# Multiplying the second norm's root onto the projections' results, and splitting the input inside the residual block

## The chip, the cores and the metric

The kernel runs on one core of one Trainium2 chip. The metric is the device time of one launch in microseconds; the median of repeated executions is compared. All data are float32. Products of matrices are made in three passes over values that are split into a high half and a low half, so that nearly the full precision is kept.

## The reference, cut to what matters

Two layers of a decoder trunk work on 1024 prompt tokens and 8 sample tokens. In each layer a norm with a gain stands ahead of the mixer's input projection and another ahead of the ConvFFN:

```python
def rmsnorm(x, g):
    y = xf * lax.rsqrt(jnp.mean(xf * xf, axis=-1, keepdims=True) + EPS)
    return y * g

h = rmsnorm(x, norm_mix_pre[layer])
proj = h @ w_in                      # 24 tiles of 128 columns (25 in layer 0)
...                                  # mixer, then mix = ... @ w_out
x = x + rmsnorm(mix, norm_mix_post[layer])
h = rmsnorm(x, norm_ffn_pre[layer])
g = h @ w_gate                       # then a causal convolution along the tokens
a = gelu(conv(g) + b_conv) * (h @ w_up)
x = x + rmsnorm(a @ w_down, norm_ffn_post[layer])
```

The root is one number for each token. It can be multiplied onto `h` ahead of a projection or onto the projection's result.

## The kernel before, in words

The activations lie transposed: 128 channels on the partitions, 1032 tokens (1024 and 8) in a row, eight such tiles `T.acc[:, k, :]` for the 1024 channels. The matrix product of such tiles with a weight tile of 128 columns takes 72 matmuls (8 tiles k, three passes, three chunks of 344 tokens) and fills one of two regions of PSUM, three banks each. `T.hh` and `T.hl` hold the high and low halves of the eight input tiles, `slot_h` and `slot_l` those of four weight tiles.

Every engine has its own program, written out by hand, and waits on semaphores. The work is a row of blocks; a block ends for all engines at once. Four blocks of the kind `stage_norm` are followed by a block that reads the normed input: `nm0` and `nm1` (first norm of a layer) by `stage_project`, `nf0` and `nf1` (second norm of a layer) by `stage_ffn`. `stage_norm` in three of the four (not in `nm0`, where there is no residual yet) does this:

- TensorE sums the squares of the mixer's or ConvFFN's result over the channels (`ones_times`, L128), ScalarE makes the root `rstd` (L135, L136).
- For each tile k: VectorE (even k, L325) or GpSimd (odd k, L338) multiplies with `rstd`; VectorE multiplies with the gain and adds the old x (L329), which gives the new x and counts up `x_new`.
- ScalarE squares the new tile (L313), TensorE adds it to the sum of squares, and SyncE stores it (L297). From k = 4 on, ScalarE makes the high half of one weight tile ahead of each square (L379), and GpSimd its low half (L383).
- ScalarE makes the second root, in `T.sqsum`. That ends the block.

The next block begins with `StageInput`: VectorE multiplies a tile with gain and root into one of two buffers (`scale`, L245), ScalarE makes its high half (L235), VectorE (odd k) or GpSimd (even k) its low half (L239). TensorE's first product follows tile by tile (`ready`). Only then does the stage run at its steady pace. ScalarE is in `stage_project` otherwise busy with splitting weights and, in layer 0, with activations.

In `stage_project` VectorE moves each finished product out of PSUM (`move`, L627). In `stage_ffn` there are eleven groups. TensorE makes, for two tiles t of the hidden layer, the gate (region 0) and the up product (region 1), and after the first pair eight products of the group before with `w_down`, two of these tiles each. Per tile, ScalarE copies the gate out of PSUM (`tile`, L739), VectorE convolves it (five instructions, L879 to L885), ScalarE applies the gelu (L743), VectorE multiplies with the up product from PSUM (L891) and splits the result into halves (L896, L897). VectorE also adds the eight down products to `T.acc` (`collect`, L904). The last group's down products start only when its second tile is split.

Of the kernel before, what the change touches and what calls it, by code (L numbers as in the profile page):

```python
# [24 lines left out]
KD = D // P  # L25
# [191 lines left out]
class StageInput:  # L217

    def __init__(self, nc, T, name, gain_row=None):
        sem = lambda n: nc.alloc_semaphore(name + n)
        self.T, self.gain_row, self.bufs = T, gain_row, None
        self.scaled, self.hi_done = sem("scaled"), sem("hi_done")

        self.lo_done = [sem("lo_done0"), sem("lo_done1")]

    def source(self, k):
        return self.T.acc[:, k, :] if self.gain_row is None else self.bufs[k % 2]  # L230
# [6 lines left out]
    def lo_half(self, eng, k):  # L237
        eng.wait_ge(self.hi_done, k + 1)
        eng.tensor_tensor(self.T.hl[:, k, :], self.source(k), self.T.hh[:, k, :], ALU.subtract  # L239
                          ).then_inc(self.lo_done[k % 2], 1)  # L240

    def scale(self, dve, k):
        if k >= 2:
            dve.wait_ge(self.lo_done[k % 2], k // 2)
        dve.scalar_tensor_tensor(out=self.bufs[k % 2], in0=self.T.acc[:, k, :],  # L245
                                 scalar=self.T.gain[:, k, self.gain_row:self.gain_row + 1], in1=self.T.sqsum[:],
                                 op0=ALU.mult, op1=ALU.mult).then_inc(self.scaled, 1)

    def vector(self, dve):
        if self.gain_row is None:  # L250
            for k in range(KD):
                self.lo_half(dve, k)
        else:
            self.scale(dve, 0)
            for k in range(1, KD, 2):
                self.scale(dve, k)
                if k + 1 < KD:
                    self.scale(dve, k + 1)
                self.lo_half(dve, k)

    def gpsimd(self, pool):
        for k in range(0, KD if self.gain_row is not None else 0, 2):
            self.lo_half(pool, k)
# [5 lines left out]
def stage_norm(nc, T, name, post_row, x_scratch, feed):  # L269
# [3 lines left out]
    with ExitStack() as ctx:  # L273
# [4 lines left out]
        root1, normed, act_own = sem("root1"), sem("normed"), sem("act_own")  # L278
# [4 lines left out]
        with nc.Block() as block:  # L283
# [17 lines left out]
            def _(act):  # L301
# [16 lines left out]
            def _(dve):  # L318
                steps = Steps(dve, dve_own)

                if post:
                    dve.wait_ge(root1, 1)
                    for k in range(KD):
                        if k % 2 == 0:
                            steps.done(dve.tensor_tensor(T.acc[:, k, :], T.acc[:, k, :], rstd[:], ALU.mult))  # L325
                        else:
                            dve.wait_ge(normed, k // 2 + 1)
# [3 lines left out]
                                                 in1=xold[:, k % 4, :], op0=ALU.mult, op1=ALU.add).then_inc(x_new, 1)  # L331

            @block.gpsimd
            def _(pool):
                if post:
                    pool.wait_ge(root1, 1)
                    for k in range(1, KD, 2):
                        pool.tensor_tensor(T.acc[:, k, :], T.acc[:, k, :], rstd[:], ALU.mult).then_inc(normed, 1)  # L338
                feed.first_gpsimd(pool)
# [72 lines left out]
def stage_project(nc, T, name, source, feed, m_tiles, out_scratch=None, tail=None, conv=None):  # L412
# [9 lines left out]
    with ExitStack() as ctx:  # L422
# [4 lines left out]
        source.bufs = [out[:, r, PAD:] for r in range(2)]  # L427
# [31 lines left out]
        with nc.Block() as block:  # L459
# [48 lines left out]
            def _(pool):  # L508
# [22 lines left out]
                source.gpsimd(pool)  # L531
# [13 lines left out]
            def _(act):  # L545
# [20 lines left out]
                for k in range(KD):  # L566
                    source.scalar(act, k)
                    if not fed and k >= KD - feed.SLOTS:
# [14 lines left out]
            def _(pe):  # L583
                def tile(j, i):
# [5 lines left out]
                    for k in range(KD):  # L590
                        if j == 0:
                            source.ready(pe, k)
# [23 lines left out]
            def _(dve):  # L616
                def move(j, i):
# [9 lines left out]
                    dve.tensor_copy(chunks(dst), region(T.ps, j % 2)).then_inc(moved[j], 1)  # L627
# [30 lines left out]
                source.vector(dve)  # L658
                dve.wait_ge(source.lo_done[0], KD // 2)
# [17 lines left out]
def stage_ffn(nc, T, name, source, feed, layer, w_down, w_conv, b_conv, state, out_prompt, out_sample):  # L677
# [3 lines left out]
    with ExitStack() as ctx:  # L681
# [21 lines left out]
        source.bufs = [gate[:, 2:2 + TOK], conv[:]]  # L703
# [3 lines left out]
        with nc.Block() as block:  # L707
# [23 lines left out]
            def _(act):  # L731
# [20 lines left out]
                def group(g, more):  # L752
                    tile(0, g)
# [6 lines left out]
                    tile(1, g)  # L760
# [6 lines left out]
                for k in range(KD):  # L767
                    source.scalar(act, k)
# [10 lines left out]
            def _(pool):  # L779
# [20 lines left out]
                source.gpsimd(pool)  # L800
                pool.wait_ge(source.scaled, KD)
# [3 lines left out]
                group(GROUPS - 1, False)  # L805
                pool.memset(T.sqsum[:], 0.0).then_inc(sqsum_own, 1)
# [5 lines left out]
            def _(pe):  # L812
                def hidden(s, g):
                    pe.wait_ge(lo[s], g + 1)
                    for k in range(KD):
                        if s == 0 and isinstance(g, int) and g == 0:
# [1638 lines left out]
```

## Time and profile before

| | |
|---|---|
| median of 3 runs | 3521.66 us (3521.66 to 3524.58) |
| span of the profiled execution, first to last instruction | 3518.7 us |
| TensorE, busy | 3038.9 us (86%) |
| VectorE, busy | 1600.2 us (45%) |
| ScalarE, busy | 935.1 us (27%) |
| GpSimd, busy | 913.4 us (26%) |
| mean granted TensorE clock | 0.921 |

For the profiled execution only the span is known; the median is 2.96 us more, which is the time around the first and the last instruction. Busy time counts an instruction from its start to its end, also while it waits for a port, and a matmul's end is modelled.
### The profile page before, as it was taken

All of it is one profiled execution on the core that took longest, in us unless ns stands there. A gap on an engine that the chain in (4) does not pass through costs nothing. (4 is left out here: it accounts for less than half of the span.)

```text
span 3518.7 us, 46382 instructions
## 1 busy us (share of the span) xinstructions
PE 3038.9 (86%) x18726; PEld 2906.3 (83%) x18726; DVE 1600.2 (45%) x1858; ACT 935.1 (27%) x1342; POOL 913.4 (26%) x474
## 2 busy tenths in 40 slices
PE   7999478959699999999689956777596999999995
PEld 6999368839599999999579956666494999999995
DVE  3263435432555444444531127777326444444444
ACT  3221433212321211211320015666213212111112
POOL 2221034304432212221422103333045222122113
PEclk9999689969799999999899978888798999999997
DMA  4221300021411111110322122122304111111103
GB/s 161 90 96 52 135 9 0 1 78 48 160 37 61 46 36 54 54 36 12 112 88 96 71 96 96 60 89 72 120 26 160 49 60 36 36 60 48 36 12 98
DMA packets 158134, 235.94 MB, mean 67 GB/s; under 512 B 12625, under 2 KB 124625, under 8 KB 157976
## 3 DMA queue, kind: packets, MB, share of 16 engines
q1 hardware_dynamic: 158060, 234.95, 19.7%
q8 instruction: 46, 0.75, 0.1%
q14 instruction: 28, 0.23, 0.0%
HBM read 176.75 MB, written 58.46 MB: 67 GB/s over the span
## 5 line engine op out<-in xcount | busy, mean ns | idle before, releaser
L904 DVE TENSOR_TENSOR acc<-acc,ps 128x1032 f32<-128x1032 f32 x176 | 216.3, 1229 | 292.1 <-PE ps L119 292.1
L119 PE MATMUL ps<-ffn_in1hi,rest1wh 128*128 128x344 f32 x1056 | 226.0, 323 | 4.2 <-DVE ffn_in1lo L239 3.5
L119 PE MATMUL ps<-ffn_in0hi,rest0wh 128*128 128x344 f32 x1056 | 225.5, 322 | 3.2 <-DVE ffn_in0lo L239 2.9
L119 PE MATMUL ps<-ffn_in1lo,rest1wh 128*128 128x344 f32 x1056 | 225.1, 321 | 0.0
L119 PE MATMUL ps<-ffn_in0lo,rest0wh 128*128 128x344 f32 x1056 | 224.9, 321 | 0.0
L119 PE MATMUL ps<-ffn_in0hi,rest0wl 128*128 128x344 f32 x1056 | 223.8, 320 | 0.0
L119 PE MATMUL ps<-ffn_in1hi,rest1wl 128*128 128x344 f32 x1056 | 223.8, 320 | 0.0
L383 POOL TENSOR_TENSOR rest0wl<-wraw,rest0wh 128x1024 fp32r<-128x1024 f32 x52 | 130.6, 2516 | 306.9 <-ACT rest0wh L379 306.8
L383 POOL TENSOR_TENSOR rest1wl<-wraw,rest1wh 128x1024 fp32r<-128x1024 f32 x52 | 130.4, 2512 | 265.3 <-ACT rest1wh L379 265.0
L119 PEld LDWEIGHTS ps<-ffn_in1hi,rest1wh 128*128 128x128 f32 x1056 | 178.5, 189 | 5.4 <-DVE ffn_in1lo L239 4.1
L119 PEld LDWEIGHTS ps<-ffn_in0hi,rest0wh 128*128 128x128 f32 x1056 | 178.4, 189 | 4.1 <-DVE ffn_in0lo L239 3.5
L119 PEld LDWEIGHTS ps<-ffn_in1lo,rest1wh 128*128 128x128 f32 x1056 | 179.9, 190 | 0.0
L119 PEld LDWEIGHTS ps<-ffn_in0lo,rest0wh 128*128 128x128 f32 x1056 | 179.5, 190 | 0.0
L119 PEld LDWEIGHTS ps<-ffn_in1hi,rest1wl 128*128 128x128 f32 x1056 | 176.8, 189 | 0.0
L119 PEld LDWEIGHTS ps<-ffn_in0hi,rest0wl 128*128 128x128 f32 x1056 | 176.7, 189 | 0.0
L2111 POOL TENSOR_TENSOR wraw<-at_s,at_rc 128x128 f32<-128x128 f32 (+3 forms) x64 | 76.7, 1198 | 256.5 <-DVE at_rc L2055 250.4
L627 DVE COPY poout<-ps 128x1032 f32<-128x1032 f32 x24 | 29.6, 1233 | 234.9 <-PE ps L119 234.9
L119 PE MATMUL ps<-mix_in1hi,in1wh 128*128 128x344 f32 x576 | 123.7, 323 | 13.8 <-POOL mix_in1lo L239 9.1
L119 PE MATMUL ps<-mix_in0hi,in0wh 128*128 128x344 f32 x600 | 129.3, 324 | 4.8 <-DVE mix_in0lo L239 4.4
L119 PE MATMUL ps<-mix_in0lo,in0wh 128*128 128x344 f32 x600 | 128.3, 322 | 0.0
L119 PE MATMUL ps<-mix_in0hi,in0wl 128*128 128x344 f32 x600 | 127.5, 321 | 0.0
L119 PE MATMUL ps<-mix_in1lo,in1wh 128*128 128x344 f32 x576 | 123.0, 322 | 0.0
(434 smaller groups left out, 6871.1 us busy)
## 6 DMA issues: line engine op xcount, KB each, us to landing
wraw<-in_w_ffn_gate SPq DMA_DIRECT2D x22, 1024.0 KB, 5.4
wraw<-in_w_ffn_up SPq DMA_DIRECT2D x22, 1024.0 KB, 5.3
wraw<-in_w_ffn_down SPq DMA_DIRECT2D x22, 1024.0 KB, 4.9
x_scratch<-acc SPq DMA_DIRECT2D x32, 516.0 KB, 7.8
proj_odd<-poout SPq DMA_DIRECT2D x24, 516.0 KB, 2.7
wraw<-in_w_in_even SPq DMA_DIRECT2D x12, 1024.0 KB, 5.6
wraw<-in_w_in_odd SPq DMA_DIRECT2D x12, 1024.0 KB, 5.6
sr_page<-in_cache_k SPq DMA_DIRECT2D x16, 512.0 KB, 5.5
```

The lines of the kernel that those rows point to most:

```text
L119: ins = pe.matmul(ps[:, 3 * r + c, 0:CH], w, h[:, c * CH:(c + 1) * CH], start=first and n == 0, stop=last and n == 2)
L383: pool.tensor_tensor(self.slot_l[j], self.source(j), self.slot_h[j], ALU.subtract).then_inc(self.lo[j], 1)
L627: dve.tensor_copy(chunks(dst), region(T.ps, j % 2)).then_inc(moved[j], 1)
L904: dve.tensor_tensor(a, a, region(T.ps, m % 2), ALU.add).then_inc(collected, 1)
L2111: pool.tensor_tensor(w[:, i % 2, 0:spans[i]], s[:, i % 4, 0, 0:spans[i]], rc[:, i % 4, 0:1].to_broadcast([P, spans[i]]), ALU.mult).then_in ...
```

## The change

The gain is applied when the new x is split, inside `stage_norm`; the second root is multiplied onto the results of the projections. ScalarE makes the high half of `gain * x` directly ahead of the square; VectorE makes the low half one tile later. VectorE also takes over GpSimd's four multiplications with `rstd`. In `stage_project` the copy out of PSUM becomes a multiplication with the root. In `stage_ffn` VectorE takes the gate out of PSUM, with the root, in place of ScalarE, and multiplies the product of gelu and up once more with the root ahead of its split. GpSimd clears `T.acc` at once and `T.sqsum` only after the last split.

```diff
 class StageInput:
     def scalar(self, act, k):
-        if self.gain_row is not None:
-            act.wait_ge(self.scaled, k + 1)
-        act.activation(self.T.hh[:, k, :], self.source(k), ACT.Copy).then_inc(self.hi_done, 1)
         if self.gain_row is None:
+            act.activation(self.T.hh[:, k, :], self.T.acc[:, k, :], ACT.Copy).then_inc(self.hi_done, 1)
         else:
+            act.activation(self.T.hh[:, k, :], self.T.acc[:, k, :], ACT.Copy, scale=self.gain(k)).then_inc(self.hi_done, 1)
+    def vector(self, dve, k):
+        dve.wait_ge(self.hi_done, k + 1)
+        ...
+            ins = dve.scalar_tensor_tensor(out=self.T.hl[:, k, :], in0=self.T.acc[:, k, :], scalar=self.gain(k),
+                                           in1=self.T.hh[:, k, :], op0=ALU.mult, op1=ALU.subtract)
+        ins.then_inc(self.lo_done[k % 2], 1)
...
 def stage_norm(...):                      # ScalarE
                     if post:
                         act.wait_ge(x_new, k + 1)
+                    source.scalar(act, k)
                     if k >= 2:
                         act.wait_ge(summed2, k - 1)
                     act.activation(sq[:, k % 2, :], T.acc[:, k, :], ACT.Square).then_inc(squared, 1)
...                                        # VectorE
-                        if k % 2 == 0:
-                            steps.done(dve.tensor_tensor(T.acc[:, k, :], T.acc[:, k, :], rstd[:], ALU.mult))
-                        else:
-                            dve.wait_ge(normed, k // 2 + 1)
+                        steps.done(dve.tensor_tensor(T.acc[:, k, :], T.acc[:, k, :], rstd[:], ALU.mult))
                         dve.wait_ge(x_in[k % 4], 16 * (k // 4 + 1))
                         dve.scalar_tensor_tensor(...).then_inc(x_new, 1)
+                        if k:
+                            source.vector(dve, k - 1)
+                else:
+                    for k in range(KD - 1):
+                        source.vector(dve, k)
+                source.vector(dve, KD - 1)
...                                        # GpSimd
-                if post:
-                    pool.wait_ge(root1, 1)
-                    for k in range(1, KD, 2):
-                        pool.tensor_tensor(T.acc[:, k, :], T.acc[:, k, :], rstd[:], ALU.mult).then_inc(normed, 1)
...
 def stage_project(...):                   # VectorE
-                    dve.tensor_copy(chunks(dst), region(T.ps, j % 2)).then_inc(moved[j], 1)
+                    if fed:
+                        dve.tensor_tensor(chunks(dst), chunks(T.sqsum[:]), region(T.ps, j % 2), ALU.mult).then_inc(moved[j], 1)
+                    else:
+                        dve.tensor_copy(chunks(dst), region(T.ps, j % 2)).then_inc(moved[j], 1)
...
 def stage_ffn(...):                       # ScalarE
-                def tile(t, g):
-                    act.wait_ge(made[2 * t], g + 1)
-                    act.wait_ge(kept, 2 * g + t)
-                    act.wait_ge(conved, 2 * g + t)
-                    act.activation(chunks(gate[:, 2:2 + TOK]), region(T.ps, 0), ACT.Copy).then_inc(gate_in, 1)
...                                        # GpSimd
-                pool.wait_ge(source.scaled, KD)
                 pool.memset(T.acc[:], 0.0).then_inc(acc_zero, 1)
...
+                pool.wait_ge(a_ready, 2 * GROUPS)
                 pool.memset(T.sqsum[:], 0.0).then_inc(sqsum_own, 1)
...                                        # VectorE
                 def convolve(steps, t, g):
+                    dve.wait_ge(made[2 * t], g + 1)
+                    dve.wait_ge(kept, 2 * g + t)
+                    dve.tensor_tensor(chunks(gate[:, 2:2 + TOK]), chunks(T.sqsum[:]), region(T.ps, 0), ALU.mult
+                                      ).then_inc(gate_in, 1)
                     dve.wait_ge(gate_in, 2 * g + t + 1)
...
                 def split(steps, t, g):
                     dve.wait_ge(multiplied, 2 * g + t + 1)
+                    steps.done(dve.tensor_tensor(conv[:], conv[:], T.sqsum[:], ALU.mult))
                     steps.done(dve.tensor_copy(ah[:, t, :], conv[:]))
```

The calls of `source.scalar`, `source.vector`, `source.gpsimd` and `ready` at the start of `stage_project` (for a normed input) and of `stage_ffn` are gone, and with them `scale`, `lo_half` and the two buffers.

## Rows read from the trace of the kernel before

**Rows 1.** Windows: stretch | us, busy us of PE, PEld, DVE, ACT, POOL, granted clock, DMA.

```profile
1166.00:1266.00 100.00, 100.00 (x635) 100.00 (x634) 50.63 (x36) 16.78 (x14) 20.32 (x10) 1.00 0.13 42
```

**Rows 2.** Timeline, second norm of layer 0: start, us, engine, line, instruction [idle before].

```profile
905.76 1.23 DVE L325 TENSOR_TENSOR acc<-acc,nf0rstd 128x1032 f32<-128x1032 f32 x1 [10.96 <-ACT nf0rstd L136]
...
907.03 6.58 DVE L329 SCALAR_TENSOR_TENSOR acc<-acc,gain,nf0xold 128x1032 f32<-128x1032 f32 x2
...
923.57 2.56 POOL L383 TENSOR_TENSOR rest0wl<-wraw,rest0wh 128x1024 fp32r<-128x1024 f32 x1 [4.41 <-ACT rest0wh L379]
...
928.40 6.59 DVE L329 SCALAR_TENSOR_TENSOR acc<-acc,gain,nf0xold 128x1032 f32<-128x1032 f32 x2
```

**Rows 3.** Timeline of VectorE in the output stage, GpSimd idle.

```profile
3501.80 1.22 DVE L2369 TENSOR_TENSOR acc<-acc,out_rstd 128x1032 f32<-128x1032 f32 x1
...
3505.47 1.23 DVE L2369 TENSOR_TENSOR acc<-acc,out_rstd 128x1032 f32<-128x1032 f32 x1
```

**Rows 4.** Timeline, end of the second norm of layer 0 and start of its ConvFFN.

```profile
935.02 1.06 ACT L313 ACTIVATE nf0sq<-acc 128x1032 f32<-128x1032 f32 x1 [1.30 <-DVE acc L329]
...
936.14 2.00 PE L128 MATMUL ps<-nf0sq,con_sb 128*128 128x344 f32 x6 [1.30 <-ACT nf0sq L313]
...
941.97 1.29 DVE L245 SCALAR_TENSOR_TENSOR ffn0gate<-acc,gain,sqsum 128x1032 f32<-128x1032 f32 x1 [6.98 <-PEq L283]
```

**Rows 5.** Timeline of TensorE, the sum ahead of that norm's first root.

```profile
898.42 3.78 PE L128 MATMUL ps<-sqsum,con_sb 128*128 128x344 f32 x6 [5.01 <-PEq L459]
```

**Rows 6.** Timeline, first norm of layer 0 and start of its projection.

```profile
24.63 16.91 PE L128 MATMUL ps<-nm0sq,con_sb 128*128 128x344 f32 x48 [3.59 <-ACT nm0sq L313]
...
37.48 1.05 ACT L379 ACTIVATE in0wh<-wraw 128x1024 fp32r<-128x1024 f32 x1
...
38.43 1.05 ACT L313 ACTIVATE nm0sq<-acc 128x1032 f32<-128x1032 f32 x1
...
45.38 1.29 DVE L245 SCALAR_TENSOR_TENSOR peout<-acc,gain,sqsum 128x1032 f32<-128x1032 f32 x1 [23.94 <-PEq L283]
...
50.01 1.20 PE L119 MATMUL ps<-mix_in0hi,in0wh 128*128 128x344 f32 x3
...
53.52 0.63 PE L119 MATMUL ps<-mix_in0lo,in0wh 128*128 128x344 f32 x3
```

**Rows 7.** Timeline of TensorE, first tile of both ConvFFNs.

```profile
948.89 1.23 PE L119 MATMUL ps<-ffn_in0hi,rest0wh 128*128 128x344 f32 x3
...
952.50 1.06 PE L119 MATMUL ps<-ffn_in0lo,rest0wh 128*128 128x344 f32 x3
...
953.36 1.06 PE L119 MATMUL ps<-ffn_in0hi,rest0wl 128*128 128x344 f32 x3
...
965.43 0.73 PE L119 MATMUL ps<-ffn_in0hi,rest0wh 128*128 128x344 f32 x3 [1.75 <-DVE ffn_in0lo L239]
...
2718.89 0.95 PE L119 MATMUL ps<-ffn_in1hi,rest1wh 128*128 128x344 f32 x3 [1.78 <-DVE ffn_in1lo L239]
...
2723.36 0.64 PE L119 MATMUL ps<-ffn_in1hi,rest1wh 128*128 128x344 f32 x3
```

**Rows 8.** The page's costliest groups: the projections' eviction from PSUM (busy us, mean ns | idle).

```profile
L627 DVE COPY poout<-ps 128x1032 f32<-128x1032 f32 x24 | 29.6, 1233 | 234.9 <-PE ps L119 234.9
```

**Rows 9.** Timeline, one steady ConvFFN group of layer 0.

```profile
1183.37 1.23 DVE L904 TENSOR_TENSOR acc<-acc,ps 128x1032 f32<-128x1032 f32 x1 [1.62 <-PE ps L119]
...
1185.37 5.69 DVE L897 TENSOR_TENSOR ffn0al<-ffn0conv,ffn0ah 128x1032 fp32r<-128x1032 f32 x1
...
1194.73 1.04 ACT L739 ACTIVATE ffn0gate<-ps 128x1032 f32<-128x1032 f32 x1 [9.45 <-PE ps L119]
...
1217.58 1.28 ACT L739 ACT_TABLE_LOAD   x1 [10.37 <-PE ps L119]
...
1228.83 1.23 DVE L891 TENSOR_TENSOR ffn0conv<-ffn0conv,ps 128x1032 f32<-128x1032 f32 x1 [2.83 <-PE ps L119]
```

**Rows 10.** Timeline of TensorE, last product of the ConvFFN, layer 0.

```profile
1687.53 0.71 PE L119 MATMUL ps<-ffn0ah,rest0wh 128*128 128x344 f32 x3 [3.48 <-DVE ffn0al L897]
```

More of the change, by code:

```diff
@@ L223, in __init__ @@
         sem = lambda n: nc.alloc_semaphore(name + n)
[L224 to L230, printed above, removed]
-    def scalar(self, act, k):
-        if self.gain_row is not None:
-            act.wait_ge(self.scaled, k + 1)
-        act.activation(self.T.hh[:, k, :], self.source(k), ACT.Copy).then_inc(self.hi_done, 1)
@@ L237, in lo_half @@
[L237 to L247, printed above, removed]
@@ L249, in vector, with gain @@
-    def vector(self, dve):
+        self.T, self.gain_row = T, gain_row
+        self.hi_done, self.lo_done = sem("hi_done"), [sem("lo_done0"), sem("lo_done1")]
+    def gain(self, k):
+        return self.T.gain[:, k, self.gain_row:self.gain_row + 1]
+    def scalar(self, act, k):
         if self.gain_row is None:
-            for k in range(KD):
-                self.lo_half(dve, k)
-        else:
-            self.scale(dve, 0)
-            for k in range(1, KD, 2):
[L256 to L259, printed above, removed]
@@ L261, in gpsimd @@
-    def gpsimd(self, pool):
-        for k in range(0, KD if self.gain_row is not None else 0, 2):
-            self.lo_half(pool, k)
+            act.activation(self.T.hh[:, k, :], self.T.acc[:, k, :], ACT.Copy).then_inc(self.hi_done, 1)
+        else:
+            act.activation(self.T.hh[:, k, :], self.T.acc[:, k, :], ACT.Copy, scale=self.gain(k)).then_inc(self.hi_done, 1)
+    def vector(self, dve, k):
+        dve.wait_ge(self.hi_done, k + 1)
+        if self.gain_row is None:
+            ins = dve.tensor_tensor(self.T.hl[:, k, :], self.T.acc[:, k, :], self.T.hh[:, k, :], ALU.subtract)
+        else:
+            ins = dve.scalar_tensor_tensor(out=self.T.hl[:, k, :], in0=self.T.acc[:, k, :], scalar=self.gain(k),
+                                           in1=self.T.hh[:, k, :], op0=ALU.mult, op1=ALU.subtract)
+        ins.then_inc(self.lo_done[k % 2], 1)
@@ L426, in stage_project @@
         squares = TileSquares(sem, T, [out[:, r, PAD:] for r in range(2)]) if out_scratch is None else None
-        source.bufs = [out[:, r, PAD:] for r in range(2)]
         fed = source.gain_row is not None
@@ L564, in iteration @@
                             activate(j, i - 1, conv.BEFORE)
-                for k in range(KD):
+                for k in range(0 if fed else KD):
                     source.scalar(act, k)
-                    if not fed and k >= KD - feed.SLOTS:
+                    if k >= KD - feed.SLOTS:
                         feed.hi_half(act, k - (KD - feed.SLOTS), 0)
@@ L590, in tile @@
                     for k in range(KD):
-                        if j == 0:
+                        if j == 0 and not fed:
                             source.ready(pe, k)
@@ L626, in move @@
                             dve.wait_ge(stored[j + 2], 16 * i)
-                    dve.tensor_copy(chunks(dst), region(T.ps, j % 2)).then_inc(moved[j], 1)
+                    if fed:
+                        dve.tensor_tensor(chunks(dst), chunks(T.sqsum[:]), region(T.ps, j % 2), ALU.mult).then_inc(moved[j], 1)
+                    else:
+                        dve.tensor_copy(chunks(dst), region(T.ps, j % 2)).then_inc(moved[j], 1)
                 def convolve(steps, j, i):
@@ L656, in iteration @@
                             convolve(steps, j, i)
-                source.vector(dve)
-                dve.wait_ge(source.lo_done[0], KD // 2)
+                for k in range(0 if fed else KD):
+                    source.vector(dve, k)
                 if conv is not None:
@@ L674, in ffn_feed, with stage_ffn @@
     return WeightFeed(nc, T, name, (w_gate, w_up), lambda b, g: 256 * g, lambda j: j % 2, lambda j: j // 2)
-def stage_ffn(nc, T, name, source, feed, layer, w_down, w_conv, b_conv, state, out_prompt, out_sample):
+def stage_ffn(nc, T, name, feed, layer, w_down, w_conv, b_conv, state, out_prompt, out_sample):
     ROWS = 2 * SAMPLES + 4
@@ L765, in group @@
                         split(3, g + 1)
-                for k in range(KD):
-                    source.scalar(act, k)
                 with act.Fori(0, GROUPS - 1) as g:
@@ L2396, in trunk_step @@
                     feed = projection_feed(nc, T, f"in{layer}", ins["w_in_even" if layer == 0 else "w_in_odd"][0])
-                    stage_norm(nc, T, f"nm{layer}", (None, 6)[layer], x_t, feed)
                     source = StageInput(nc, T, f"h{layer}", layer)
+                    stage_norm(nc, T, f"nm{layer}", (None, 6)[layer], x_t, feed, source)
                     if layer == 0:
@@ L2415, in trunk_step @@
                     feed = ffn_feed(nc, T, f"ffn{layer}w", ins["w_ffn_gate"][layer], ins["w_ffn_up"][layer])
-                    stage_norm(nc, T, f"nf{layer}", 2 + layer, x_t, feed)
                     source = StageInput(nc, T, f"hf{layer}", 4 + layer)
-                    stage_ffn(nc, T, f"ffn{layer}", source, feed, layer, ins["w_ffn_down"][layer], ins["w_ffn_conv"][layer],
+                    stage_norm(nc, T, f"nf{layer}", 2 + layer, x_t, feed, source)
+                    stage_ffn(nc, T, f"ffn{layer}", feed, layer, ins["w_ffn_down"][layer], ins["w_ffn_conv"][layer],
                               ins["b_ffn_conv"][layer:layer + 1], ins["state_ffn_conv"], outs["ffn_conv_prompt"],
```

18 lines of the change are left out of this document (4 added, 14 removed).

## The prediction, made before the changed kernel ran

> **What bounds the kernel now.** I read the page's shares first: TensorE 86%, nobody else over 45%. Then the windows, to see where the missing 14% lie. In a steady ConvFFN group TensorE is busy for 100.00 of 100 us at full clock, while VectorE has half its time free [rows 1]; the projections look the same once they run. So an edit can only count where TensorE waits. Then the timeline from a norm's root to the end of the first product behind it, in all four norms. There the engines follow one another: VectorE and GpSimd share the residual work, the second root is made, and only then is the input scaled and split, with TensorE following tile by tile. The last such place is the end of each ConvFFN, where TensorE waits for VectorE's split [rows 10]. I call "block start" the start of the block behind a norm.
>
> **The residual block (three norms).** First what one VectorE instruction costs. From a multiplication by the root to the gain-and-add behind it is 907.03 - 905.76 = 1.27 us [rows 2]. With GpSimd idle, one multiplication and two gain-and-adds take 3505.47 - 3501.80 = 3.67 us [rows 3], so one gain-and-add takes (3.67 - 1.27) / 2 = 1.20. Beside GpSimd two of them take 6.58 instead of 2.5 [rows 2]: each GpSimd instruction holds VectorE up by 6.58 / 2 - 1.25 = 2.04 us. Check on the whole: four multiplications, eight gain-and-adds and seven holds (four of GpSimd's multiplications, three weight halves) are 5.1 + 9.6 + 14.3 = 29.0; measured from 905.76 to 928.40 + 6.59 = 934.99 it is 29.2.
>
> After the change, up to the last gain-and-add: 8 x 1.27 + 8 x 1.20 = 19.8, six low halves ahead of it, and the holds of GpSimd's weight halves. A low half in this new form is in no row. The form with the same inputs costs 1.20, a plain subtraction at most 3.4 beside GpSimd, which is a hold counted apart; I take 1.20: 7.2. All four weight halves come before the last gain-and-add by my order of ScalarE's work (the fourth stands behind square 6, and VectorE has a low half, a multiplication and the gain-and-add of tile 7 left then): 4 x 2.04 = 8.2; were they all late, 0. Sum 35.2, that is +6.0 against 29.2. GpSimd's saving (four holds, 8.2) is less than the VectorE work that comes in (four multiplications 5.1, six halves 7.2), and the fourth weight half (2.0) now falls inside.
>
> Behind the last gain-and-add ScalarE now makes a high half ahead of the square: +1.0 (a tile of this size takes 1.06 [rows 4]; scaled by a column it could be 1.2). Then TensorE sums in 2.00 us [rows 4], because its tiles came close together. Now tile 7 follows tile 6 after two to four VectorE instructions and a hold or two; TensorE is idle for some 4 to 6 us. After 5.01 us of idle the same sum takes 3.78 at the low clock [rows 5]. I take that: +1.8; the other end is 0. Store of x: it ended before the roots did, and ends before them again. Together +8.8 per norm, 26.4 for three.
>
> The Trainium skill, "TensorE: Matmul & The Clock Gate", Part 1, says that the throttled clock is the default and only activity releases it; that speaks against this change, since it thins out the sums. Without it (sums stay at 2.00) the total below would be 5.3 lower.
>
> **The first norm (no residual).** TensorE's eight sums run without a gap from 24.63 for 16.91 us, to 41.54 [rows 6]; ScalarE waits for them. After the change ScalarE has 20 instructions and not 12. Its first square is one instruction later, and from the fourth tile on it starts three instructions per tile, 38.43 - 37.48 = 0.95 us apart [rows 6], 2.85 against TensorE's 2.0. Up to tile 3 TensorE still sets the pace, at the low clock first: sum 0 ends near 29.1 (1.0 for the high half, then 3.5), sum 1 near 31.6, and square 3 waits for it and ends at 32.6. Twelve more instructions at 0.95 end at 44.0, the last sum at 46.1: +4.6. Were ScalarE never held up, it would be +3; with TensorE at 3.5 all along, +12. VectorE's eight halves and GpSimd's four run beside that, in 18 us at most.
>
> **The blocks behind.** Block start to the start of the eighth k of the first product is 965.43 - 941.97 = 23.46 us [rows 4, 7], and the same within 0.05 in the other three; 1.42 more to its end, 24.9. Afterwards all halves are there. Nine matmuls at the low clock take three times 953.36 - 952.50 = 0.86 [rows 7], so 0.287 each; at full clock eighteen take 2.85 (eviction to eviction, 1.23 and the idle 1.62 [rows 9]), 0.158 each. The low stretch lasted from 948.89 to about 954: 18 slow, 54 fast, 5.1 + 8.5 = 13.6 us.
> - ConvFFN: TensorE still starts 948.89 - 941.97 = 6.9 us into the block [rows 4, 7], since it first transposes rows that a transfer brings. So 6.9 + 13.6 = 20.5, gain 4.4. In layer 1 there is a second low stretch that the waits bring about: eighteen matmuls take 2723.36 - 2718.89 = 4.47 instead of 2.9 [rows 7]. Without waits it goes, gain 5.9.
> - Projection of layer 0: start 50.01 - 45.38 = 4.6 in, again transposes [rows 6]; the low stretch ends by 53.52, where three matmuls take 0.63 instead of 1.06 [rows 6], some 0.9 us less of loss, so 12.7: gain 24.9 - 17.3 = 7.6.
> - Projection of layer 1: no transposes, it starts at once: gain 24.9 - 13.6 = 11.3. Is the clock still up there, up to 2 more; I don't count on it.
>
> Gains 29.2.
>
> **The steady stages.** A move out of PSUM costs 1.233 as a copy [rows 8] and 1.23 as an operation with an SBUF input [rows 9]: nothing. In a ConvFFN group VectorE gets 2 x (1.23 + 1.27) = 5 us more of 68; it has to be free where the chain passes.
> - Tile 0: the gate left PSUM by ScalarE after a table load of 1.28 at 1217.58 [rows 9] and a copy of 1.04; VectorE does it in 1.23, so the convolution begins a good 1 us earlier. Up to the multiplication at 1228.83 nothing is added. The table load moves to the weight half.
> - Tile 1: VectorE's split of tile 0 ends at 1185.37 + 5.69 = 1191.06 [rows 9], plus 1.27 is 1192.3; the gate is ready at 1194.7. 2.4 us of cover. If gone, 1 us late is 1 us at most in each of 22 groups, and only once the convolution's own slack of some 3 us is spent.
> - GpSimd's clearing of `T.acc` is early and covered; that of `T.sqsum` waits for the last split, but its first use comes some 6 us later.
>
> **The end of each ConvFFN.** The last down product starts 3.48 us after its predecessor, released by VectorE's low half [rows 10]. One multiplication goes in: +1.27, twice 2.5. The clock is low there in any case.
>
> **Sum.** 26.4 + 4.6 + 2.5 - 29.2 = +4.3: span 3523.0, and with the 2.96 us around it 3525.9. The changed kernel gives the overlap back as a longer block ahead of it.
>
> The Trainium skill, "SBUF — State Buffer", section "Who interferes with whom", says that a GpSimd instruction that reads SBUF and a VectorE instruction with two SBUF inputs lock each other out for the whole instruction. A weight half is 2.56 long [rows 2] and costs VectorE 2.04; were it the whole, the twelve holds would cost 6 us more than in my sum.
>
> **The rivals.**
> - A, the clock is kinder: the last sums run at 2.00 and the first product's low stretch is shorter. For it: the tiles 0 to 3 of each norm come regularly. Against it: 5.01 us of idle was enough for the low clock. -5.3 - 1: 3519.6.
> - B, faster: the weight halves of GpSimd fall behind the last gain-and-add. It decides on whether ScalarE gets to the third and fourth weight half before VectorE's last pair. Two holds fewer in three norms are 12.2 us: 3513.7. Against it: ScalarE has slack between two tiles.
> - C, slower, a second low stretch: with TensorE's sums thinned out, each first product or its neighbour has one more, as layer 1 has before. Its price is 4.47 - 2.9 = 1.6, at four places and the two ends: +8 to 10, 3534.5. It decides on how long TensorE is idle ahead of the block.
> - D, slower, VectorE becomes the bound in the ConvFFN: a further hold of 2 to 4.5 us in the split of tile 0 (5.69 instead of 1.23 is one such [rows 9]) makes the gate of tile 1 late. Some 1 us in 20 groups: 3546. Against it: 2.4 and then 3 us of slack.
>
> **How the numbers follow.** Chances: my sum 0.49 (its own range 3521 to 3531), A 0.14, B 0.11, C 0.18, D 0.06, something else 0.02. No change can be told within 0.2%, 7 us, so from 3514.6 to 3528.7. Faster: B, 0.11. Slower: C and D, and a quarter of my own case, 0.35. Same: 0.54. The range 3515 to 3535 leaves out D, the outer parts of B and C.
>
> **What would show it.** From the first root's use to the last gain-and-add about 35 us instead of 29, with holds by the four weight halves alone; the last sum at 3.8 instead of 2.0; block start some 9 us later after the root; first product without gaps, 13 to 14 us long; steady ConvFFN at 100%; TensorE idle 4.7 instead of 3.48 ahead of the last down products. I am wrong if VectorE passes the residual block in under 33 us, if the steady groups show idle time, or if the first product starts at full clock.

## The result, and the profile after

The changed kernel takes 3530.03 us (median of 18 runs, 3524.69 to 3534.28), the kernel before 3522.43 (18 runs): ratio 1.002, 95% interval 1.0013 to 1.0027. It is 7.6 us slower. Forecast were +4.3 us and a range of 3515 to 3535. The profiled execution has a span of 3529.8 us, 11.1 more than before.

What lies around the span is less than the 2.96 us that stood for it before the prediction: the profiled execution of the changed kernel took 3531.59 us, 1.8 more than its span. With 1.8 us around it, the profiled execution of the kernel before took about 3520.5 us (an estimate), some 1.9 less than the median of 3522.43, and that of the changed kernel 1.6 more than its own. So 3.5 of the 11.1 us come from which executions were profiled.

The steady stages did not move. Windows of the changed kernel, one steady stretch of the first ConvFFN [rows 1]:

```profile
1166.00:1266.00 100.00, 100.00 (x634) 100.00 (x633) 57.19 (x40) 14.04 (x11) 22.74 (x9) 1.00 0.10 32
```

TensorE is busy throughout, VectorE has 57 us of work instead of 51. The move out of PSUM with the root costs what the copy did [rows 8] (from the costliest groups of the profile's page):

```profile
L604 DVE TENSOR_TENSOR poout<-sqsum,ps 128x1032 f32<-128x1032 f32 x24 | 29.5, 1229 | 254.2 <-PE ps L119 254.2
```

In this document the residual block is the stretch in which the multiplications by the first root and the gain-and-adds run. A hold is the time by which a VectorE instruction beside a GpSimd instruction takes longer than alone. Timeline of VectorE in the second norm of layer 0 [rows 2]:

```profile
907.54 1.23 DVE L303 TENSOR_TENSOR acc<-acc,nf0rstd 128x1032 f32<-128x1032 f32 x1 [10.96 <-ACT nf0rstd L136]
...
908.81 1.29 DVE L305 SCALAR_TENSOR_TENSOR acc<-acc,gain,nf0xold 128x1032 f32<-128x1032 f32 x1
...
923.53 3.38 DVE L239 SCALAR_TENSOR_TENSOR ffn_in0lo<-acc,gain,ffn_in0hi 128x1032 fp32r<-128x1032 f32 x1
...
926.84 3.38 DVE L303 TENSOR_TENSOR acc<-acc,nf0rstd 128x1032 f32<-128x1032 f32 x1
...
935.13 3.40 DVE L239 SCALAR_TENSOR_TENSOR ffn_in0lo<-acc,gain,ffn_in0hi 128x1032 fp32r<-128x1032 f32 x1
...
938.45 3.38 DVE L303 TENSOR_TENSOR acc<-acc,nf0rstd 128x1032 f32<-128x1032 f32 x1
...
941.86 1.29 DVE L305 SCALAR_TENSOR_TENSOR acc<-acc,gain,nf0xold 128x1032 f32<-128x1032 f32 x1
```

From the first multiplication to the end of the last gain-and-add it is 943.15 - 907.54 = 35.6 us; before it was 29.2. The four rows of 3.4 us are those that GpSimd's four weight halves hold up; all others take 1.2 to 1.3. The first two of these weight halves (GpSimd; the other two start at 934.71 and 938.39):

```profile
923.10 2.72 POOL L361 TENSOR_TENSOR rest0wl<-wraw,rest0wh 128x1024 fp32r<-128x1024 f32 x1 [23.33 <-ACT rest0wh L357]
926.78 2.35 POOL L361 TENSOR_TENSOR rest0wl<-wraw,rest0wh 128x1024 fp32r<-128x1024 f32 x1 [0.96 <-ACT rest0wh L357]
```

What follows on ScalarE, the high half of tile 7 and the start of the second root [rows 4]:

```profile
943.19 1.16 ACT L232 ACTIVATE ffn_in0hi<-acc,gain 128x1032 fp32r<-128x1032 f32 x1 [4.88 <-DVE acc L305]
...
949.20 1.12 ACT L135 ACTIVATE sqsum<-ps,eps 128x1032 f32<-128x1032 f32 x1 [2.60 <-PE ps L128]
```

And on TensorE: the sum ahead of the first root and that of tile 7 [rows 4, 5], then the transposes and the first product of the ConvFFN [rows 7]:

```profile
900.20 3.78 PE L128 MATMUL ps<-sqsum,con_sb 128*128 128x344 f32 x6 [5.01 <-PEq L436]
...
945.36 3.81 PE L128 MATMUL ps<-nf0sq,con_sb 128*128 128x344 f32 x6 [5.01 <-ACT nf0sq L292]
...
957.41 1.89 PE L809 MATMUL ps<-con_sb,wraw 20*128 20x20 f32 x16 [8.25 <-DMA ffn0more_rows<-in_b_ffn_conv]
...
959.88 1.23 PE L119 MATMUL ps<-ffn_in0hi,rest0wh 128*128 128x344 f32 x3
...
962.62 0.92 PE L119 MATMUL ps<-ffn_in0hi,rest0wh 128*128 128x344 f32 x3
...
963.38 0.63 PE L119 MATMUL ps<-ffn_in0lo,rest0wh 128*128 128x344 f32 x3
```

The last sum takes 3.81 us as the one at 900.20 does, and no longer 2.00. The first product has no gap; groups of three matmuls start 0.86 us apart up to 962.62 (the low clock) and 0.47 from 963.38 on. I call the time for which TensorE works at the low clock behind idle time a low stretch; this one lasts 3.3 us. In the projection of layer 1 the first product starts with the block, also at the low clock (TensorE):

```profile
1785.26 1.20 PE L119 MATMUL ps<-mix_in1hi,in1wh 128*128 128x344 f32 x3 [4.16 <-PEq L261]
...
1788.83 0.83 PE L119 MATMUL ps<-mix_in1lo,in1wh 128*128 128x344 f32 x3
```

VectorE at the split of tile 0 in a steady group [rows 9]: the split ends at 1198.06 and the gate is ready at 1200.68, so VectorE waits 2.6 us for it (forecast 2.4): the added work is covered.

```profile
1191.80 4.99 DVE L866 CAST ffn0ah<-ffn0conv 128x1032 fp32r<-128x1032 f32 x1
...
1196.83 1.23 DVE L867 TENSOR_TENSOR ffn0al<-ffn0conv,ffn0ah 128x1032 fp32r<-128x1032 f32 x1
...
1200.68 1.23 DVE L842 TENSOR_TENSOR ffn0gate<-sqsum,ps 128x1032 f32<-128x1032 f32 x1 [2.62 <-PE ps L119]
```

TensorE at the end of the first ConvFFN [rows 10]: idle 4.75 instead of 3.48 us, then a low stretch of 5.8 us, up to 1700.50.

```profile
1694.70 1.20 PE L119 MATMUL ps<-ffn0ah,rest0wh 128*128 128x344 f32 x3 [4.75 <-DVE ffn0al L867]
...
1700.00 0.87 PE L119 MATMUL ps<-ffn0ah,rest0wh 128*128 128x344 f32 x3
```

The two spans, taken apart at the same instructions in both traces:

| stretch | forecast | measured |
|---|---|---|
| three residual norms, first root to second root (35.94 before, 45.18 after) | +26.4 | +27.7 |
| first norm, first ScalarE instruction to the root (20.50, 25.33) | +4.6 | +4.8 |
| root to the second move of the projection's result, layer 0 (37.94, 31.28) | -7.6 | -6.7 |
| root to the first up product taken, ConvFFN of layer 0 (37.96, 32.84) | -4.4 | -5.1 |
| root to the last move, projection of layer 1 (287.96, 276.53) | -11.3 | -11.4 |
| root to the first up product taken, ConvFFN of layer 1 (39.52, 32.95) | -5.9 | -6.6 |
| first to last up product taken, each ConvFFN (705.59, 705.59) | 0 | 0.0 |
| last up product to last collect, both ConvFFNs (28.00 and 27.90; 30.33 and 30.38) | +2.5 | +4.8 |
| everything that no edit touches | 0 | +3.6 |
| sum | +4.3 | +11.1 |

Without the last line but one it is +7.5, close to the difference of the medians, 7.6. The untouched stages (loading the input +2.1, the first mixer +1.5) differ as much between two profiles of one kernel: in a second profile of the kernel before, with a span of 3522.7 us, loading took 1.2 us and the first mixer 2.8 us more than in its first.

### The profile page after: what moved, and what is told of

The parts are those of the page before. It is cut to its first block and busy times, and to the rows that moved or that the text cites. A ratio compares the mean times of both kernels' runs of the same rounds, so it can differ in the third digit from the quotient of the medians.

```text
span 3529.8 us, 46392 instructions
## 1 busy us (share of the span) xinstructions
PE 3038.3 (86%) x18726; PEld 2904.8 (82%) x18726; DVE 1711.2 (48%) x1942; ACT 893.3 (25%) x1298; POOL 844.9 (24%) x446
## 5 line engine op out<-in xcount | busy, mean ns | idle before, releaser
L604 DVE TENSOR_TENSOR poout<-sqsum,ps 128x1032 f32<-128x1032 f32 x24 | 29.5, 1229 | 254.2 <-PE ps L119 254.2
```

Of the source, the lines that this page charges most:

```text
L604: dve.tensor_tensor(chunks(dst), chunks(T.sqsum[:]), region(T.ps, j % 2), ALU.mult).then_inc(moved[j], 1)
```

## The experiments

Each ratio is against the kernel before, run on the same chip beside the kernel in question; its medians there were 3522.7 to 3524.05. "Less than the changed kernel" compares with the median 3530.03, from another set of runs. The edits shown are cut; `...` stands for lines left out.

**GpSimd's weight halves behind the last gain-and-add.**

```diff
 def stage_norm(...):                      # GpSimd
-                feed.first_gpsimd(pool)
+                if post:
+                    pool.wait_ge(x_new, KD)
+                    for j in range(2):
+                        feed.lo_half(pool, j, 0)
+                else:
+                    feed.first_gpsimd(pool)
...                                        # slots 2 and 3 at the start of the block behind
```

> The changed kernel, with GpSimd's low halves of the first weight tiles moved: in the three norms with a residual the first two come after the last gain-and-add, the other two at the start of the block behind. Theory (VectorE's chain sets the block, and each of these GpSimd instructions holds it up by 2.04 us): from the first use of the root to the end of the last gain-and-add 27.4 us instead of 35.6, because four holds of 2.04 go; the new tiles then come every 3.7 us and the last sum of squares runs at the full clock, 2.0 instead of 3.8. Together 3 x (8.2 + 1.8) = 30 us less than the changed kernel (which stands at 1.002 of the kernel before), so a ratio of about 0.994. Rival 1 (the clock stays low at the last sum): 3 x 8.2 = 24.5 less, 0.995. Rival 2 (paid in the tail): two GpSimd halves of 2.4 and two low halves of 1.2 between them last 7.2 us or more behind the last gain-and-add, the block waits for them, and less than 10 us is left of the gain: above 0.999.

3500.06 us, ratio 0.9929 (0.9915 to 0.9942). Its second norm of layer 0 (VectorE, then GpSimd, then TensorE):

```profile
907.62 1.23 DVE L303 TENSOR_TENSOR acc<-acc,nf0rstd 128x1032 f32<-128x1032 f32 x1 [10.96 <-ACT nf0rstd L136]
...
923.60 1.29 DVE L239 SCALAR_TENSOR_TENSOR ffn_in0lo<-acc,gain,ffn_in0hi 128x1032 fp32r<-128x1032 f32 x1
...
933.41 1.29 DVE L305 SCALAR_TENSOR_TENSOR acc<-acc,gain,nf0xold 128x1032 f32<-128x1032 f32 x1
...
934.62 4.59 DVE L239 SCALAR_TENSOR_TENSOR ffn_in0lo<-acc,gain,ffn_in0hi 128x1032 fp32r<-128x1032 f32 x2
...
934.79 6.63 POOL L366 TENSOR_TENSOR rest0wl<-wraw,rest0wh 128x1024 fp32r<-128x1024 f32 x2 [34.94 <-DVE acc L305]
...
936.90 2.00 PE L128 MATMUL ps<-nf0sq,con_sb 128*128 128x344 f32 x6 [1.67 <-ACT nf0sq L292]
```

The last gain-and-add ends at 934.70, 27.1 us after the first multiplication, each of the six low halves ahead of it takes 1.28 or 1.29, and the last sum 2.00; in the other two norms it is 27.1 and 2.00 too. Both parts of the theory came, 30 us less than the changed kernel; rival 2 did not, since GpSimd's two halves end at 941.42, ahead of the block's end at 942.7.

**The square ahead of the high half.** In ScalarE's loop `source.scalar(act, k)`, the instruction that makes the high half, moves behind the square.

> The changed kernel, with ScalarE squaring a new tile ahead of its high half and not behind it. Theory (the high half lies on the path to the second root): the last high half, 1.06 us, goes from the path in all four norms, 4 us in total less than the changed kernel: ratio 1.001 to the kernel before. Rival (VectorE's low half waits for the high half now, and its delay passes to the next multiplication): the low half of tile k-1 stands behind the gain-and-add of tile k, 2.5 us later than the tile it belongs to, so a wait of up to 0.3 us per tile comes in and nothing is gained: 1.002.

3529.01 us, ratio 1.0014 (1.0005 to 1.0023), 1.0 less than the changed kernel in the medians, inside what they can tell. In the trace, first root to second root takes 44.13 instead of 45.18 us in each of the three norms and the first norm 0.7 less: the high half does lie on the path, 1.05 us of it. The rival did not come: VectorE's chain takes 35.6 us as before. As a time of the whole kernel this stays inconclusive.

**The second multiplication by the root on the gelu's output.**

```diff
                 def multiply(steps, t, g):
                     dve.wait_ge(activated, 2 * g + t + 1)
+                    steps.done(dve.tensor_tensor(conv[:], conv[:], T.sqsum[:], ALU.mult))
                     dve.wait_ge(made[2 * t + 1], g + 1)
...
                 def split(steps, t, g):
-                    steps.done(dve.tensor_tensor(conv[:], conv[:], T.sqsum[:], ALU.mult))
```

> The changed kernel, with VectorE's second multiplication by the root in the ConvFFN placed on the gelu's output, ahead of the product with the up projection, and not behind it. Theory: in the last group VectorE waits for the up product at that time anyway, so TensorE's wait ahead of the last down products falls from 4.75 to 3.48 us, and the low stretch of the clock behind it from 5.4 to some 3.4 us: 1.27 + 1.0 in each of two layers, 4.6 less than the changed kernel, ratio 1.001. Rival 1 (the low stretch does not depend on the length of the gap): 2.5 less. Rival 2 (tile 0 of a steady group has no room: gelu ends at 1233.47 and the up product is taken at 1234.80): the multiplication of 1.27 just fits; if it does not, the product is taken late in 20 groups, and beyond 1.6 us of further cover TensorE waits: slower than the changed kernel, above 1.003.

3526.21 us, ratio 1.001 (1.0001 to 1.0019), 3.8 less. VectorE and TensorE at the end of the first ConvFFN:

```profile
1682.78 1.24 DVE L859 TENSOR_TENSOR ffn0conv<-ffn0conv,sqsum 128x1032 f32<-128x1032 f32 x1 [1.23 <-ACT ffn0conv L715]
...
1687.63 1.23 DVE L861 TENSOR_TENSOR ffn0conv<-ffn0conv,ps 128x1032 f32<-128x1032 f32 x1 [3.62 <-PE ps L119]
...
1691.00 0.94 PE L119 MATMUL ps<-ffn0ah,rest0wh 128*128 128x344 f32 x3 [3.48 <-DVE ffn0al L867]
...
1694.98 0.63 PE L119 MATMUL ps<-ffn0ah,rest0wl 128*128 128x344 f32 x3
```

The multiplication is done before the up product comes, and TensorE's idle time is 3.48 again. From the last up product to the last collect it takes 27.99 and 27.91 us, as before the change. From the first to the last up product each ConvFFN takes 705.59 us as in the changed kernel, so the steady groups lose nothing and rival 2 falls. The stretches, 4.8 us less in all, speak for the theory (4.6) and against rival 1 (2.5); the median, 3.8 less, lies between them.

**One part alone: the two projections.** `stage_norm`, `StageInput` and `stage_ffn` of the kernel before for the ConvFFNs, the changed ones for the projections.

> One part of the change alone: the root on the result and the split in the block of the norm for the two norms ahead of the input projections; both norms ahead of a ConvFFN, and the ConvFFN, as before. Theory (the terms of my sum, read after against before: -1.8 and -2.2 us at the projections, +6.5 and +5.2 at the ConvFFNs): 4 us less than the kernel before, ratio 0.9988. Rival (the loss is not in the ConvFFNs' norms, but where the two profiles differ ahead of the first norm and in the mixer, 2.1 and 1.5 us): ratio 1.001 as for the whole change.

3527.78 us, ratio 1.001 (1.0001 to 1.0019), where I expected 0.9988. The edited stretches did what the theory says: 1.8 us less at the first projection, 2.6 less at the second. But the attention stage (here all from the last move of the projection's result to the first root of the second norm, with the output projection), which nothing edits, took 613.12 us instead of 604.06.

**The other part alone: the two ConvFFNs.** The reverse.

> The other part of the change alone: the two norms ahead of a ConvFFN and the ConvFFNs changed, the two norms ahead of the input projections and the projections as before. Theory (what the two profiles show for these stages, 6.5 and 5.2 us): 11.6 us more than the kernel before, ratio 1.0033. Rival (the parts do not add up through an untouched stage, as the projections alone gave +5 and not -4): the rest of the whole, 7.6 - 5 = 2.5 us more, 1.0007.

3533.56 us, ratio 1.0034 (1.0021 to 1.0048): 10.9 us more than the kernel before, where the theory had 11.6.

**The kernel before, once more.**

> The kernel before once more, unchanged, for a second profile. Theory (the attention stage between the first projection and the second norm of layer 1, which no edit touches, takes another time in each execution): 604 us in the first profile from the last move of the projection's result to the root of the next norm; here anything from 600 to 613, at a ratio of 1.000. Rival (a kernel has its own fixed time there): 604.0 to 604.4 again.

3523.60 us, ratio 0.9996 (0.9987 to 1.0005), attention 604.12 us. In these two profiles it is as the rival says; the next run shows that such a time is not fixed.

**The projections alone, once more.**

> The kernel with the change in the two projections alone, once more, unchanged. Its edited stages were 4.3 us shorter than in the kernel before, its median 5 us longer, and its attention stage 613 us long in the profile, at a granted clock of 0.80 to 0.81 instead of 0.83. Theory (chance of the execution): attention near 605 us, ratio 0.999. Rival (this kernel's attention stage runs at the lower clock each time, though nothing in it is edited): 610 us or more again, ratio 1.001 or above.

3524.87 us, ratio 1.0007 (0.9998 to 1.0016), attention 609.95 us. Windows over the same part of the attention stage: this kernel, then its first run, then the second profile of the kernel before, then its first (the granted clock is the third number from the end):

```profile
2180.00:2430.00 250.00, 181.47 (x1009) 160.74 (x1008) 180.32 (x413) 152.42 (x368) 82.52 (x55) 0.82 0.24 84
```

```profile
2180.00:2430.00 250.00, 185.86 (x1006) 166.24 (x1006) 178.13 (x413) 152.08 (x367) 80.95 (x55) 0.80 0.24 84
```

```profile
2180.00:2430.00 250.00, 180.33 (x1029) 158.64 (x1027) 184.71 (x423) 154.09 (x372) 82.80 (x55) 0.85 0.24 84
```

```profile
2180.00:2430.00 250.00, 183.25 (x1025) 162.02 (x1024) 184.09 (x426) 154.75 (x373) 83.30 (x56) 0.83 0.23 84
```

The clock is 0.82 and 0.80, against 0.85 and 0.83, and VectorE gets through 413 instructions in 250 us instead of 423 and 426. In the profiles of nine other kernels that stage took 600.7 to 606.5 us. So the projections' part alone is not as fast as its stretches say: in both profiles an untouched stage took 6 to 9 us longer, at a lower clock. The two profiles of this one kernel are 3.2 us apart there. That the lower clock is the cause, and not a companion, of the longer stage is not shown, and why this kernel has it was not settled.

**GpSimd multiplies the odd tiles by the first root again** (its loop and the semaphore `normed` as in the kernel before).

> The changed kernel, with GpSimd doing the odd tiles' multiplications by the first root again, as in the kernel before. Theory (the port: each GpSimd instruction costs VectorE 2.04 us, its own 1.27 us would be less): from the first use of the root to the last gain-and-add 4 x 1.27 + 14 x 1.20 + 8 x 2.04 = 38.2 us instead of 35.6, so 3 x 2.6 = 8 us more than the changed kernel, ratio 1.0045. Rival (the two engines share the work and VectorE's queue gets shorter): 4 x 1.27 = 5.1 us less in each of three norms, 15 us less than the changed kernel, 0.998.

3537.56 us, ratio 1.0045 (1.0031 to 1.0059). VectorE and GpSimd in the second norm of layer 0:

```profile
905.24 1.23 DVE L304 TENSOR_TENSOR acc<-acc,nf0rstd 128x1032 f32<-128x1032 f32 x1 [10.96 <-ACT nf0rstd L136]
...
905.28 13.36 POOL L323 TENSOR_TENSOR acc<-acc,nf0rstd 128x1032 f32<-128x1032 f32 x4 [7.82 <-ACT nf0rstd L136]
...
906.51 6.59 DVE L308 SCALAR_TENSOR_TENSOR acc<-acc,gain,nf0xold 128x1032 f32<-128x1032 f32 x2
...
940.66 3.37 DVE L308 SCALAR_TENSOR_TENSOR acc<-acc,gain,nf0xold 128x1032 f32<-128x1032 f32 x1
```

From 905.24 to the end of the last gain-and-add at 944.03 it takes 38.8 us; two gain-and-adds beside GpSimd take 6.59. So it is right that VectorE does all of it: sharing costs 7.5 us more.

**The kernel before with its weight halves late.** The first experiment's edit without the change.

> The kernel before (nothing of the change), with GpSimd's low halves of the first weight tiles placed as in the run that put them late: two behind the last gain-and-add, two in the block behind, after its own low halves of the input. Theory (three of the seven holds in each residual block go): 3 x 3 x 2.04 = 18 us less than the kernel before, ratio 0.995; the change is then worth only the rest of what its version of this edit gained, 4 us. Rival (the tail pays: the halves in the block behind meet VectorE's scaling of the first tile there): less than 9 us gained, above 0.9975, and the change is worth 14 us or more once the halves are out of its way.

3520.20 us, ratio 0.9991 (0.9982 to 1.0001), 2.5 us less than the kernel before, a gain that the interval cannot tell from nothing. That is not the theory's 18 us but what the rival says, less than 9. Its second norm of layer 0 (VectorE, TensorE, ScalarE):

```profile
911.48 1.23 DVE L325 TENSOR_TENSOR acc<-acc,nf0rstd 128x1032 f32<-128x1032 f32 x1 [10.96 <-ACT nf0rstd L136]
...
933.49 1.29 DVE L329 SCALAR_TENSOR_TENSOR acc<-acc,gain,nf0xold 128x1032 f32<-128x1032 f32 x1 [0.17 <-DMA nf0xold<-x_scratch]
...
927.12 13.64 PE L128 MATMUL ps<-nf0sq,con_sb 128*128 128x344 f32 x36 [3.47 <-ACT nf0sq L313]
...
940.79 1.12 ACT L135 ACTIVATE sqsum<-ps,eps 128x1032 f32<-128x1032 f32 x1 [0.79 <-PE ps L128]
```

VectorE does lose three holds: 934.78 - 911.48 = 23.3 us instead of 29.2. But then TensorE's sums, 36 matmuls without a gap to 940.76, set the root, and from first to second root only 3.1 of the 5.9 us are left (3.9 and 4.2 in the other two norms). Behind the block, the first up product is taken 43.0 us after the root instead of 38.0; by the last up product half of that is made up, and 2.5 us remain. Change and edit go together: with both the kernel is 22.7 us faster than the kernel before; alone the change costs 7.6, and the edit gains 2.5 in the medians, which may be nothing and at most 6.

**TensorE kept at work in the gaps.**

```diff
                     ones_times(pe, T, 1, sq[:, k % 2, :], ...).then_inc(summed2, 1)
+                    if post and k in (4, 6):
+                        for n in range(6):
+                            pe.matmul(T.ps[:, n % 3, 0:CH], T.con[:, C_ONE:C_ONE + P], T.con[:, 0:CH],
+                                      start=True, stop=True)
```

> The changed kernel, with twelve recorded matmul passes (4.0 us at the full clock, on constants, into banks that nobody reads any more) added on TensorE behind the sums of tiles 4 and 6 in the three norms with a residual, where TensorE is otherwise idle for some 6 us. Theory (the last sum takes 3.8 instead of 2.0 us only because the clock has fallen in that idle time): tiles 5 and 7 are summed in 2.0 us, 1.8 us of the path to the second root go in each of three norms, 5.4 less than the changed kernel, ratio 1.0005. Rival (the extra work runs into the tile that follows, or the clock falls all the same): nothing gained or a few us lost, 1.002 to 1.003.

3527.65 us, ratio 1.0013 (1.0004 to 1.0022), 2.4 less; against the kernel before beside it, it is 3.7 us more where the changed kernel was 7.6 more. TensorE in the second norm of layer 0, added work at L328:

```profile
925.67 2.00 PE L128 MATMUL ps<-nf0sq,con_sb 128*128 128x344 f32 x6 [1.67 <-ACT nf0sq L292]
...
927.51 3.63 PE L328 MATMUL ps<-con_sb 128*128 128x344 f32 x12
...
933.62 2.00 PE L128 MATMUL ps<-nf0sq,con_sb 128*128 128x344 f32 x6 [2.47 <-ACT nf0sq L292]
...
945.23 3.08 PE L128 MATMUL ps<-nf0sq,con_sb 128*128 128x344 f32 x6 [2.46 <-ACT nf0sq L292]
```

Tile 5 is summed in 2.00 us here, but in 3.65 and 3.48 in the other two norms, in spite of the added work. Tile 7 takes 3.08 here and 2.00 in the other two norms; first root to second root falls from 45.18 to 44.46, 43.38 and 43.38 us, 4.3 us in all against 5.4 expected. As a time the size is between theory and rival. The cause of the long last sum is shown: the sum goes from 3.81 to 2.00 us, and the path with it by 1.80, where nothing changed but TensorE's work in the gap.

**All three edits together.**

> The changed kernel with three edits together: GpSimd's low halves of the weights behind the last gain-and-add, the square ahead of the high half, the root on the gelu's output. Theory (the three sit on different parts of the path and add up): 30 + 4 + 4.6 = 39 us less than the changed kernel, about 3491 us, ratio 0.991 to the kernel before. Rival (GpSimd's two halves end only 1.3 us ahead of the block's end in the first of these kernels, so the 1.06 us of the high half is not gained, and the noise of the untouched mixers hides the rest): no better than 30 us less, 0.993.

3492.47 us, ratio 0.9917 (0.9903 to 0.9930), 37.6 us less than the changed kernel against 39 expected. This is the fastest kernel run, 30 us faster than the kernel before. As a time it does not show that all three add up: the stretches from root to root (34.08 us, 0.77 less than with the weight halves alone) and the ends of the ConvFFNs (28.00 and 27.99 us) do.

## Why the prediction was right, point by point

- **The residual block** (+8.8 forecast per norm, +9.2 measured). VectorE's chain 35.2 against 35.6, all four weight halves inside it, each worth 2.10 to 2.14 (my "at most 3.4" for a plain subtraction beside GpSimd overlooked the 5.69 of [rows 9], but in these three blocks no VectorE instruction took longer than 3.40); high half +1.06; last sum 3.81 where I took 3.78. Shown by moving the halves (27.1 us, 2.00), by putting GpSimd's multiplications back (38.8) and by keeping TensorE at work. Rivals A and B fall: the last sum was slow, and no hold fell behind the last gain-and-add by itself.
- **The first norm** +4.8 against +4.6.
- **The blocks behind** -29.8 against -29.2. Each term is within 1 us: the low stretch in the projection of layer 0 lasted 5.2 us where I had 3.5, in the two ConvFFNs 3.3 and 3.5 where I had 5.1 (read off the kernel before, where it was 5.7). That these errors cancel is luck: over the profiles of all kernels, where a first product started at the low clock its low stretch lasted anything from 2.9 to 6.1 us, a difference of some 1.4 us in time (an estimate: eleven matmuls at 0.287 instead of 0.158 us). No second low stretch came (rival C), and the one of layer 1 went.
- **Steady stages** 0.0 in both ConvFFNs, with 2.6 us of cover at tile 1. Rival D falls.
- **The end of each ConvFFN** is the term that was mis-sized: +4.8 against +2.5. The idle time was as forecast, 4.75 us. But "the clock is low there in any case" put at nothing that the low stretch can be longer: 5.8 us here, where with 3.48 us of idle it was 3.4. With 3.48 us of idle the stretch from the last up product to the last collect took 27.9 to 28.0 us in seven profiles; with 4.75 us it took 29.0 to 29.3 in some and 30.2 to 30.4 in others. So the upper value is not a price of every run: the error of 2.3 us is this size in the profile shown and would have vanished with the shorter low stretch. TensorE of the kernel with the square first, same idle time, low stretch of 3.0 us and not 5.8:

```profile
1695.46 1.20 PE L119 MATMUL ps<-ffn0ah,rest0wh 128*128 128x344 f32 x3 [4.75 <-DVE ffn0al L867]
...
1698.18 0.77 PE L119 MATMUL ps<-ffn0ah,rest0wh 128*128 128x344 f32 x3
```

- **The sign.** I gave 0.54 to no change and 0.35 to slower; the sum of my terms without that one error would have been +6.6, and 7.6 is just beyond the 7 us that I had taken as the bound. So by the median the outcome that I held most likely did not come, though the sum had the right sign; the interval of the ratio, 1.0013 to 1.0027, reaches to both sides of that bound, 1.002. The bound was too coarse: 18 runs tell this change from nothing, and would tell a smaller one too. None of my three signs of being wrong showed: the residual block took 35.6 us and not under 33, the steady groups had no idle time, and every first product started at the low clock.
- **The two rules.** The Trainium skill, "TensorE: Matmul & The Clock Gate", Part 1 (throttled by default, released by activity), holds at the last sum: 3.81 us, and 2.00 in two of three norms where TensorE was kept at work. The Trainium skill, "SBUF — State Buffer", section "Who interferes with whom", calls the use of the shared ports "an exclusive lock", held "for the whole instruction" where it speaks of VectorE's two-port modes; by that a hold here would last as long as the GpSimd instruction. Measured are 2.10 to 2.14 us per hold beside GpSimd records of 2.35 to 2.73. The profile's times of GpSimd are rough, so this does not refute the rule, but the measured cost is the one to sum with.

## What to carry to other kernels

Moving work out of a serial stretch and into a block ahead of it gains nothing when the block's own chain takes it in on the same engine: sum both sides, here -29.8 and +32.5. Look then for what else sits in that chain without belonging to it; four GpSimd instructions on weights, due later, cost VectorE 8.5 us per norm and, through TensorE's clock, 1.8 more, and moving them turned +7.6 into -22.7 us. Try the same edit without the change, too: alone it gave 2.5, not clear of the noise, because TensorE's sums were the next bound in the block.

## What was not expected of the hardware

- The same idle time of 4.75 us was followed by a low stretch of 3.0 us in one kernel and of 5.8 in another. The kernel with TensorE kept at work had both in one execution: 30.4 us from the last up product to the last collect in layer 0, 29.2 in layer 1. At this place the times of all kernels fall into two groups some 1.2 us apart; at the first products the low stretch took any length from 2.9 to 6.1 us.
- A stage that no edit touches (attention) took 604.06 and 604.12 us in two profiles of the kernel before, but 613.12 and 609.95 in two of a kernel that differs only elsewhere, at a granted clock of 0.80 to 0.82 instead of 0.83 to 0.85. With parts of a change of 4 us, the stretches of the trace told more than the medians.
